# Moving filler products and small steps in a two-block transformer kernel: transposes ahead of the third quarter, two quarters in five late slots, the second group's output product behind three quarters

## What is computed

```python
u = _rms_norm(h, g_pre)
cols = u @ w_in                       # q, k, v, z of attention; r, k, v, z of the recurrence; two gates
y_a = softmax(q k^T + bias) v * silu(z_a)          # 8 heads of 64
y_b = groupnorm(scan over time of r, decay, k, v, a) + bonus
y_b = y_b * silu(z_b)                              # 8 heads of 64
merged = sigmoid(gate_a) * (y_a @ p_a) + sigmoid(gate_b) * (y_b @ p_b)
y = merged @ w_out
h = h + rms_norm(y, g_post)
h = h + sigmoid(h @ w_ple_gate) * (p @ w_ple_up)
```

## Time and profile before

| | |
|---|---|
| median of 3 runs | 888.42 us (888.45, 885.73, 888.42) |
| the profiled execution, its own time | 884.25 us |
| its span, first to last instruction | 882.2 us |
| TensorE busy / VectorE / ScalarE | 98% / 76% / 54% of the span |
| granted TensorE clock, mean | 0.996 of full speed |
| slots 8 to 16 | 702.97 us to 772.4 us |
| behind the slots, up to w_out | 772.4 us to 823.6 us |

### The profile page before, as it was taken

The page is one execution under the profiler, slowest core; times in us unless marked ns, Lnnn a source line. Parts: engine busy times, 40 slices in busy tenths (PEclk is TensorE's granted clock), DMA queues, the critical chain, the costliest instruction groups (busy, mean ns, idle before and its releaser), DMA issues. The chain is left out here.

```text
span 882.2 us, 19228 instructions
## 1 busy us (share of the span) xinstructions
PE 861.0 (98%) x7612; PEld 786.7 (89%) x7612; DVE 669.9 (76%) x996; ACT 480.5 (54%) x775; POOL 119.8 (14%) x136
## 2 busy tenths in 40 slices
PE   7999999999999999999999999999999989898998
PEld 7999888888889988888888888899999979797998
DVE  6996887777667876778877767786998676567775
ACT  5774565555445576655555554459613554373463
POOL 2003300000122000050000017630007200000110
PEclk9999999999999999999999999999999999998999
DMA  9542555554556533155555455674443543333451
GB/s 341 193 169 104 171 187 186 185 188 142 189 196 224 192 116 111 61 191 191 190 190 188 163 162 183 214 271 144 144 144 100 136 130 94 124 114 138 140 195 48
DMA packets 23410, 144.50 MB, mean 164 GB/s; under 512 B 2968, under 2 KB 3224, under 8 KB 9648
## 3 DMA queue, kind: packets, MB, share of 16 engines
q1 hardware_dynamic: 22032, 140.26, 46.2%
q0 software_dynamic: 1168, 3.23, 1.6%
q10 hardware_dynamic: 144, 0.06, 0.0%
HBM read 142.47 MB, written 1.06 MB: 163 GB/s over the span
## 5 line engine op out<-in xcount | busy, mean ns | idle before, releaser
L2150 DVE TENSOR_TENSOR lo<-raw,hi 128x1024 fp32r<-128x1024 f32 (+1 forms) x210 | 244.1, 1205 | 11.4 <-ACT hi L1540 8.3
L609 PE MATMUL ps<-X,hi 128*128 128x512 f32 x704 | 221.1, 395 | 0.0
L596 PE MATMUL ps<-X,hi 128*128 128x256 f32 x600 | 173.1, 289 | 0.2
L597 PE MATMUL ps<-X,hi 128*128 128x256 f32 x600 | 169.7, 283 | 0.0
L598 PE MATMUL ps<-X,lo 128*128 128x256 f32 x600 | 169.7, 283 | 0.0
L606 PEld LDWEIGHTS ps<-X,lo 128*128 128x128 f32 x704 | 132.0, 188 | 33.4 <-issue 1.9
L606 PE MATMUL ps<-X,lo 128*128 128x256 f32 x704 | 139.5, 279 | 1.1 <-DVE X L2165 1.0
L1540 ACT ACTIVATE hi<-raw 128x1024 fp32r<-128x1024 f32 (+1 forms) x109 | 107.7, 988 | 27.1 <-DMA raw<-in_down 13.6
L596 PEld LDWEIGHTS ps<-X,hi 128*128 128x128 f32 x600 | 114.9, 191 | 3.8 <-issue 2.7
L597 PEld LDWEIGHTS ps<-X,hi 128*128 128x128 f32 x600 | 115.0, 192 | 0.4 <-issue 0.2
L598 PEld LDWEIGHTS ps<-X,lo 128*128 128x128 f32 x600 | 115.0, 192 | 0.0
(11 more groups left out here) (443 smaller groups left out, 1442.3 us busy)
## 6 DMA issues: line engine op xcount, KB each, us to landing
raw<-in_wide SPq DMA_DIRECT2D x106, 1024.0 KB, 5.0
raw<-in_down SPq DMA_DIRECT2D x32, 704.0 KB, 4.1
BI<-bias_table POOLq DMA_DIRECT2D x16, 128.0 KB, 5.1
raw<-in_wide SPq DMA_DIRECT2D x3, 512.0 KB, 8.6
X<-in_x SPq DMA_DIRECT2D x1, 1024.0 KB, 12.7
WG<-in_group SPq DMA_DIRECT2D x1, 768.0 KB, 16.9
out<-X SPq DMA_DIRECT2D x3, 256.0 KB, 2.4
cmask<-in_masks POOLq DMA_DIRECT2D x1, 544.0 KB, 6.3
```

The source lines that it names most:

```text
L596: nc.tensor.matmul(dst, wh, xh, start=first, stop=False, skip_group_check=True)
L597: nc.tensor.matmul(dst, wh, xl, start=False, stop=False, skip_group_check=True)
L609: return nc.tensor.matmul(bank, wh, x, start=False, stop=last, skip_group_check=True)
L2150: nc.vector.tensor_tensor(lo[:, s, a:b], raw[:, s, a:b], hi[:, s, a:b].bitcast(F32), ALU.subtract).then_inc(lo_ready, 1)
```

## The change

The order of the list is changed in five places, and one activation moves:

- in the slots with transposes (`TURNS`: 8, 10, 13, 15), `mturn` now stands behind the second quarter and ahead of what is left of the share. In slots 13 and 15 nothing is left of it, in slots 8 and 10 one quarter;
- slots 11 to 15 get two quarters each (before 3, 3, 2, 3, 3), slot 16 gets three. The units they would have used move behind slot 16;
- slot 16 holds `yt` of group 0 alone, then its three quarters, `gate_sig(0, 4)` and then `yt` of group 1;
- `gn3` and `gn4` move from the middle of units 127 and 128 to between the quarters of units 125 and 126, and `gate_sig` is cut 4 and 4 where it was 5 and 3;
- `z_silu` moves from slot 8 to slot 10, and the Silu of unit 118 goes with it (`gate_silu(1)`).

The number and kind of instructions stay the same, but for table loads on ScalarE.

```diff
-                  both_groups("sa") + both_groups("state"), both_groups("yt")]
+                  both_groups("sa") + both_groups("state"), [("yt", 0)]]
...
-        SHARE = {0: 4, 13: 2, 16: 2}
+        SHARE = {0: 4, 11: 2, 12: 2, 13: 2, 14: 2, 15: 2}
...
-            second += quarters(2) + turned_in.get(n, []) + quarters(share - 2)
+            second += quarters(2) + turned_in.get(n, [])
             if n in TURNS:
                 p = TURNS.index(n)
                 second += [("mturn", 2 * p), ("mturn", 2 * p + 1)]
+            second += quarters(share - 2)
...
-            if n == 8:
+            if n == 10:
                 second += [("z_silu",)]
-        second += converted() + [("gate_sig", 0, 5)] + quarters(1)
+        second += converted() + [("gate_sig", 0, 4), ("yt", 1)] + quarters(1)
         second += both_groups("gn") + [("p_load",)] + converted() + quarters(3) + both_groups("gn2") + [("own_out",)] + converted()
-        second += quarters(len(fills_)) + converted() + [("gate_sig", 5, 8)]
-        for half in range(2):
-            second += [("fill", U_PA, half)]
-        second += [("gn3", 0), ("gn4", 0), ("fill", U_PA + 1, 0), ("gn3", 1), ("gn4", 1), ("p_in",), ("fill", U_PA + 1, 1)]
+        second += quarters(3) + [("gn3", 0)] + converted() + quarters(3) + [("gn4", 0), ("gn3", 1)] + converted()
+        second += quarters(len(fills_)) + [("gn4", 1)] + converted() + [("gate_sig", 4, 8)]
+        for u in (U_PA, U_PA + 1):
+            for half in range(2):
+                second += [("fill", u, half)] + ([("p_in",)] if (u, half) == (U_PA + 1, 0) else [])
...
-                if half and part != 0 and U_ZA <= u < U_GATE:
-                    j = u - U_ZA
-                    act.wait_ge(za_in, j + 1)
-                    z = ZA[:, 2 * j:2 * j + 2, :]
-                    nc.scalar.activation(z, z, ACT.Silu).then_inc(za_done, 1)
+                if half and part != 0 and u == U_ZA:
+                    gate_silu(0)
+
+            def gate_silu(j):
+                act.wait_ge(za_in, j + 1)
+                z = ZA[:, 2 * j:2 * j + 2, :]
+                nc.scalar.activation(z, z, ACT.Silu).then_inc(za_done, 1)
...
             def z_silu():
                 act.wait_ge(shifted, 5)
+                gate_silu(1)
```

## The result

| | before | changed |
|---|---|---|
| median | 886.51 us (5 runs, 885.73 to 888.45) | 881.79 us (5 runs, 881.0 to 884.43) |
| ratio, 95% interval | | 0.9945 (0.9924 to 0.9967) |
| the profiled execution's own time | 884.25 us | 884.43 us |

The change makes the kernel faster by about 4.7 us. The forecast was 885.4 us with a range from 882.2 to 888.3; the first median lies 0.4 us under the range, the second (882.89 us) inside it.

What follows compares the result with a forecast made beforehand. TensorE, busy 98%, was taken as the bound, with 11.5 us of waits and lowered clock at stake. Terms 1.45 + 0.1 + 0.85 + 0.7, less 0.1, gave 3.0 us: 888.42 to 885.4 us, range 882.2 to 888.3.

Steps and rivals of the forecast that it cites:

- Base of the forecast: Whole kernel: the 3.0 us gain was taken from a median of 888.42 us, giving 885.4 us.
- Slot 8, +1.45 us: Slot 8: transposes a quarter earlier let the product with v start at 709.1 instead of 710.53, gaining 1.45 us.
- z_silu to slot 10: 0: ScalarE, slot 10: the moved Silu sits behind copies nobody waits for again before `apply`; costed at 0 us.
- Slot 10, +0.1 us: Slot 10: a 0.84 us wait is traded for a wait for VectorE's division, gaining 0.1 us.
- Late slots, 0: Slots 11 to 15: two quarters each still cover most of the VectorE and ScalarE chain; 0 us, ends 0 and -5.9.
- slower rival: Slots 11 to 15 lose cover, up to 1.47 us in each of four, 5.9 us: 891.3 us; chance 0.08.
- Output products parted, +0.85 us: Second group's output product: parting the groups removes a TensorE gap of 0.84 us; 0.85 us taken, ends 0 and 0.85.
- The hole: TensorE gap of 0.84 us with no releaser, inside the second group's output product, near the end of 128 small matmuls.
- The tail, +0.7 us: Units 127 to 130: 3.0 us idle ahead of unit 128 replaces 3.7 us ahead of unit 129, gaining 0.7 us.
- I take the fall and its 2.4 us as staying: Behind the 3.0 us idleness ahead of unit 128: the clock still falls to 0.50 and costs 2.4 us as before.
- The table load: ScalarE ahead of unit 128: a table load holding it longer delays unit 127's evacuation 1.4 us: 886.8 us; chance 0.05.
- The clock rival: Ahead of unit 128: the clock stays up through the 3.0 us idleness, gain 5.4 us: 883.0 us; chance 0.33.

Runs made afterwards that it cites:

- second profile: The changed kernel unaltered, run and profiled once more on another chip: 882.89 us, ratio 0.9969 to the kernel before.
- filling runs: Unread matmuls put into TensorE's idleness: 22 ahead of unit 128 in the changed kernel, ratio 0.9937; 26 ahead of unit 129 in the kernel before, 0.9972.
- order back: The changed kernel with the transposes again behind the whole share, the Silu of unit 118 staying in slot 10: ratio 0.9964 to the kernel before.
- both back: The changed kernel with transposes behind the whole share and z_silu with the Silu of unit 118 in slot 8: ratio 0.9991 to the kernel before.
- Silu back: The changed kernel with z_silu and the Silu of unit 118 in slot 8, transposes still ahead of the third quarter: ratio 0.9962 to the kernel before.
- early sigmoids: The changed kernel with the sigmoids of units 123 to 125 between ScalarE's YBH of group 0 and group 1: 878.85 us, ratio 0.9922 to the kernel before.

## Why the prediction was right and where it failed

The direction and the places were right; the sum was 3.0 us and the stages give 3.7 us from slot 8 to w_out, less 0.4 us behind it. The time missed the range by 0.4 us. Two steps failed: the base that the sum was taken from, which alone put the range too high, and the tail's term, in which the price of the lower clock was taken to stay at 2.4 us.

- **Base of the forecast.** The step that failed first is "the median gives 888.42 - 3.0". Three runs had shown 888.45, 885.73 and 888.42; with two more the median was 886.51, and in four later series it was 885.25 to 887.21. 886.51 minus the same 3.0 us gives 883.5 us, and a range 1.9 us lower, from 880.3, would have held the 881.79 us.
- **Slot 8, +1.45 us.** The size was right (1.47 in the second profile), the cause in the main wrong, so the hit was in part luck. I booked it under the order of the transposes and wrote "z_silu to slot 10: 0". Measured: 1.3 us for the Silu alone, 0.15 for the order. The working even named the Silu in front of the copies, and that it had left; the move was costed at nothing because that step looked only at who waits for the Silu, not at who stands behind it.
- **Slot 10, +0.1 us.** 0.18 measured, by the trade that was named; the wait for the division was 0.6 us, not 0.7.
- **Late slots, 0.** Measured -0.27 us in slots 14 and 15, with a wait of 0.20 us there for VectorE. The slower rival priced them at 5.9 us; they did not come near it.
- **Output products parted, +0.85 us.** The hole went and the stretch gained 0.80 us, but the run with both together has no hole either and is 0.34 us quicker. The sum took the hole for an effect of the order; what takes it away in the changed kernel isn't shown.
- **The tail, +0.7 us.** The new stall was 3.09 us where 3.0 was worked out, released by what was named. The stretch gained 1.50 us all the same: 0.6 us from the shorter stall and 0.9 us because the lower clock cost 1.54 us instead of 2.4. The step "I take the fall and its 2.4 us as staying" was the mis-sized one; the filling runs give 2.4 us in the kernel before and 1.54 in the changed one. These 0.9 us are not safe, though: both profiles of the changed kernel have them, but in two variants with the same stall gn2 to w_out took 44.7 and 44.8 us instead of 43.56, which leaves 0.3 us of the 1.50.
- **The table load.** The Trainium skill (ScalarE: Activation LUTs, What ACT_TABLE_LOAD costs) has a drain of 1.38 us beside the load, which by the prediction's estimate would have made the stall 4.4 us. The sigmoid follows the load's start by 1.29 us, 796.99 to 798.28, and the stall was 3.09: the trace agrees with the page's 1.28 us for the load, not with the drain.
- **The clock rival** (883.0 us) was nearer in number, but its mechanism didn't show: the clock fell in all six profiles of kernels with the stall of 3.1 us. A mean clock of 0.998, as two executions of the changed kernel had (880.3 and 881.1 us), doesn't speak for it: the profile with the order back had 0.998 too, and there the clock fell. Two variants with the same stall had one execution each with a mean clock of 1.000 (both back 880.58 us, Silu back 880.43 us); in these it may have stayed up, but they have no trace.
- **Not foreseen:** 0.4 to 1.6 us given back behind w_out in the two profiles of the changed kernel, where I had named XL as what might be late; SyncE's loads had been costed at nothing. It was the load of unit 135, which did not come earlier by as much as TensorE did, and a square queued behind its split. Five variants gave nothing back.

How the measured 4.7 us of the first chip divides, and why the second chip gave 2.4, isn't settled. The stages of the second profile, less the larger hole in the grams (0.6 us), give 3.7 - 0.4 - 0.6 = 2.7 us, which agrees with the second measurement but rests on one profile of each kernel; in the first the five runs of either kernel also spread by 2.7 and 3.4 us.

## What to carry to other kernels

An instruction that nobody waits for can still be the costly one: look at what stands behind it in its engine's queue, and take each part of a change back alone before its gain is credited. Where single runs spread by more than an effect, set a marker at either side of the changed code in two profiles and compare the stretches, and don't rest a forecast of 3 us on the median of three runs that spread by as much. Work moved out of a covered stretch is worth most where it becomes the cover of the next stall.

## What the runs showed of the hardware

- The clock does not fall by the length of an idleness alone. Behind 3.09 us it fell, behind 3.57 us in another variant it stayed at 1.00, behind 3.69 us it fell. In one variant (early sigmoids) it fell at 844.4 us, around short waits of 0.63 and 0.31 us beside small matmuls. It can also fall 0.8 us after TensorE has resumed. A stall of some 3 us is a risk, not a fixed price; what a fall cost, against the profiles in which the clock stayed up, was 1.3 to 2.8 us.
- 22 matmuls that nobody reads, put into an idleness that was there anyway, kept the clock up and won 1.5 us in the stages.
- TensorE's holes without a releaser are of two kinds. One was a wait for a PSUM bank, found by looking for who takes it out (1.10 us). The other breaks a run of small matmuls at a fixed instruction: 0.84 and 1.00 us in the two profiles of the kernel before, 0.84 us in both its variants, none in the thirteen profiles of the changed kernel and its variants. What decides it isn't shown.
- The mean granted clock in 8 to 20 us was 1.00, 0.86 or 0.72 in kernels that are alike there, and the grams began 636.2 to 638.9 us after the first matmul.
